# Recurrence preparation of both second-block layers moved from the mixer program into the projection program, in another row order, with key norms per token

## Chip, cores and metric

The kernel runs on one NeuronCore of a Trainium2 chip, as one launch. The metric is the device time of that launch in microseconds (us); lower is better. The time before is 3351.52 us, the median of three runs (3350.27 to 3356.59).

## The reference, cut to what matters

The program computes a first block (a state space mixer, long convolutions and a mixture over 16384 small experts) and then a second block of two layers (l = 0 and 1) on 256 tokens of width 1024. Only the second block is touched. Each of its layers projects the normed tokens to 1216 columns `za`, 416 columns `zb` and 512 columns `zc`. These feed three mixers: a gated recurrence (on za), a latent attention (on zb) and a spatial gate (on zc). After them come an output projection and a feed-forward part. What the change moves is the beginning of the recurrence, up to its loop:

```python
def rwkv7_time_mix(za, shift_mu, w0, w_up, a0, a_up, g_up, k_k, k_a, r_k, ln_g, ln_b, v_first, v0, v_down, v_up):
    za = token_shift(za, shift_mu)
    r, k, v, wd, ad, gd = jnp.split(za, A_SPLITS, axis=-1)      # 3 x 384, 32, 32, 64 columns
    w_log = -jax.nn.softplus(-(w0 + jnp.tanh(wd) @ w_up)) - 0.5
    decay = jnp.exp(-jnp.exp(w_log.astype(jnp.float32)))
    a = jax.nn.sigmoid(a0 + ad @ a_up)
    g = jax.nn.sigmoid(gd) @ g_up
    if v_first is not None:                                      # layer 1 only
        v = v + (v_first - v) * jax.nn.sigmoid(v0 + (v @ v_down) @ v_up)
    kk = heads(k * k_k)                                          # 6 heads of 64
    kk = kk / jnp.maximum(jnp.sqrt(jnp.sum(kk * kk, axis=-1, keepdims=True)), 1e-12)
    k = k * (1 + (a - 1) * k_a)
    ...                                                          # the recurrence over 256 tokens
```

## The kernel before, in words

Here l is the layer, PE the TensorE, DVE the VectorE, ACT the ScalarE, POOL the GpSimd and SP the engine whose queue issues the loads. `second_layer` (L3739) runs the layer as a chain of programs ("stages"), each with one instruction list per engine. A stage ends in a barrier over all engines (`Stage.__exit__`, L115), so no engine starts the next stage before all have finished this one. Order within an engine is the order of the code, and engines wait on each other's semaphores.

**`stage_norm_z`, the projection (L1966 to L2123).** It norms the tokens (ACT squares L2038, DVE L2082 to L2086), transposes them (PE L2014) and splits them into high and low halves hh and hl. Then it multiplies ten weight tiles "row by row": for each of the ZT = 10 tiles of 128 za columns ACT rounds the weights to a high half (L2046), DVE subtracts to get the low half (L2091), PE makes 3 x 8 matmuls (L2024), ACT evicts (L2067), and DVE applies the token shift (L2111, L2112). The tiles come in order: r (3 tiles), k (3), v (3), and last the low-rank tile (wd, ad, gd). Two tiles are in flight. After them come eight units, one for each 128 rows of depth, each with 416 columns of zb and 512 of zc (PE L2032, ACT L2054 and L2055, DVE L2095 and L2096, two units ahead). At the end ACT copies zc (L2075) and DVE zb (L2122) from PSUM.

**`stage_mixers` (L2126 to L2879).** Its first part, before PE's first `fill`, prepares the recurrence and the attention:
- ACT: gelu of zc (L2476), tanh and sigmoid of the low-rank tile (L2477, L2478), squares of the keys (L2480), sigmoids of the lifted tiles (L2484, L2485), the value gates for l = 1 (L2488 to L2491), roots (L2495, L2498), three exponentials (L2500 to L2502).
- PE: lifts of the low-rank tile (L2347), key norms as a product with a 128 x 128 matrix of ones per head (L2353), value lifts (L2359, L2363), transposes of zb (L2371), the attention's projections (L2381, L2385).
- DVE: the latent norms (L2614 to L2618, L2648 to L2652), the centring for the gate (L2621 to L2623), rope angles (L2626 to L2633), the scan over decays (L2642), a reciprocal of the 128 x 768 norms (L2658), key and removal products (L2659 to L2664), value mixing for l = 1 (L2668 to L2670), and the eight writes of AT, BT, KT and RT into block-diagonal tiles (L2678 to L2681).
- POOL: zero fill of the five block-diagonal tiles (L2268). SP: 17 or 19 loads (L2241 to L2260).

Then comes the chunked recurrence as "phases" of three PSUM banks each. PE fills a bank with four matmuls (`fill`, L2408; transposes L2406), and either DVE (`empty`, L2695, L2697) or ACT (`keep_banks`, L2541) reads it. The order is AB, NT, BH, KH, AT, V, KA, RB, RK, then five levels of W, M and T (14 phases, 42 banks), then Q, X and Z. After each bank an engine's list calls `next(attend, None)`: that issues one slice of the attention and the spatial gate ("the side work"). PE's side work is set at the first level (33 slices, first transposes L2282), DVE's at KA (L2708 onward). Between NT and KA, DVE builds the starts TT and Tm of the inverse (L2780 to L2782) and norms the heads (L2775, L2786; ACT L2535, L2548). A sequential loop over four chunks, group norms and transposes end the stage (L2444 to L2472).

Buffers: the preparation's temporaries lie in block-diagonal tiles that are used later. `shared` (L3742) holds attention data and then the output weights.

## Time and profile before

| | |
|---|---|
| median of the runs (3) | 3351.52 us |
| the profiled execution's own time / its span | 3357.79 / 3356.1 us |
| PE / DVE / ACT busy over the span | 3086.5 (92%) / 2430.1 (72%) / 1762.9 (53%) us |
| layer 0: projection / mixers | about 1462 to 1523 / 1524 to 1688.5 us |
| layer 1: projection / mixers | about 1929 to 1992 / 1994 to 2174 us |

The profile is one execution, taken by the hardware profiler. Busy times of the engines overlap, so they don't add up to the span. "Idle before" in a row is the engine's wait ahead of that group and what ended it. The weight loads (PEld) run beside the matmuls. PEclk is the clock that TensorE was granted, as a share of 2.4 GHz; 0.5 is the lower of its two levels, 1.2 GHz. The other 2900 us belong to the first block, the dense feed-forward part and the mixture of experts, which the change doesn't touch.

### The profile page before, as it was taken

The page shows a single profiled execution, that of the slowest core. Times are in us where ns is not written, and L with a number is a line of the kernel's source. Part 1 is how long each engine was busy: PE and PEld are TensorE (multiplying, and loading weights), DVE is VectorE, ACT ScalarE, POOL GpSimd, SP SyncE. Part 2 cuts the span into 40 slices and gives each one's busy share as a digit, 9 for nine tenths or more (in the row PEclk, how much of TensorE's full clock was granted, in tenths as well). Part 3 has the DMA queues.
Part 4 walks back from the last instruction along what each step waited for, and adds up shares of the span by engine and source line. Part 5 has one row for each costly group of instructions (what it writes and reads, how often), then busy time and mean ns, then how long its engine had stood idle before and what let it go on. Part 6 is the DMA issues. An engine that isn't in the chain of part 4 may idle for free. (4 is left out here: it accounts for less than half of the span.)

```text
span 3356.1 us, 49912 instructions
## 1 busy us (share of the span) xinstructions
PE 3086.5 (92%) x17008; PEld 2574.3 (77%) x17009; DVE 2430.1 (72%) x3665; ACT 1762.9 (53%) x2206; POOL 39.8 (1%) x47
## 2 busy tenths in 40 slices
PE   7999898889899999977979986879999999999997
PEld 3797546888788999965859866758888888888886
DVE  3665654899788666658645467559889888988986
ACT  3344303436533444435224344248887887888886
POOL 0000000000000000000000000000000000000000
PEclk9998798999999999988989987979999999999999
DMA  7561133345577666631135240169999999999994
GB/s 276 201 226 35 72 135 116 130 148 182 220 250 220 218 212 212 201 115 46 51 129 181 103 155 1 57 232 390 374 357 377 367 360 367 373 363 351 387 366 173
DMA packets 225998, 732.47 MB, mean 218 GB/s; under 512 B 23543, under 2 KB 59816, under 8 KB 223016
## 3 DMA queue, kind: packets, MB, share of 16 engines
q1 hardware_dynamic: 221928, 702.85, 57.2%
q0 software_dynamic: 2768, 23.59, 2.4%
q10 hardware_dynamic: 1152, 4.19, 0.3%
q8 instruction: 74, 1.21, 0.1%
q14 instruction: 76, 0.62, 0.1%
HBM read 702.76 MB, written 28.84 MB: 218 GB/s over the span
## 5 line engine op out<-in xcount | busy, mean ns | idle before, releaser
L3351 DVE TENSOR_TENSOR moe_lo<-moe_raw,moe_hi 128x1024 fp32r<-128x1024 f32 x756 | 886.1, 1220 | 66.5 <-ACT moe_hi L3201 42.7
L3201 ACT ACTIVATE moe_hi<-moe_raw 128x1024 fp32r<-128x1024 f32 x756 | 789.6, 1061 | 151.7 <-PE moe_pB L3149 83.1
L3149 PE MATMUL moe_pB<-moe_hi,moe_hEh 128*128 128x512 f32 x1008 | 399.9, 397 | 2.6 <-DVE moe_hEl L3346 2.6
L3149 PE MATMUL moe_pB<-moe_hi,moe_hEl 128*128 128x512 f32 x1008 | 394.2, 391 | 0.0
L3149 PE MATMUL moe_pB<-moe_lo,moe_hEh 128*128 128x512 f32 x1008 | 393.6, 390 | 0.0
L1547 PE MATMUL route_pS<-fh,route_uh 128*128 128x256 f32 x640 | 191.2, 299 | 36.0 <-DVE route_ul L1650 35.7
L3149 PEld LDWEIGHTS moe_pB<-moe_hi,moe_hEh 128*128 128x128 f32 x1008 | 190.0, 189 | 40.5 <-issue 2.8
L3149 PEld LDWEIGHTS moe_pB<-moe_hi,moe_hEl 128*128 128x128 f32 x1008 | 189.7, 188 | 40.7
L3149 PEld LDWEIGHTS moe_pB<-moe_lo,moe_hEh 128*128 128x128 f32 x1008 | 190.3, 189 | 38.0
L1882 PE MATMUL exp_pO<-exp_vh,exp_ah 128*128 128x512 f32 x512 | 201.1, 393 | 4.2 <-DVE exp_al L1941 4.2
L1882 PE MATMUL exp_pO<-exp_vl,exp_ah 128*128 128x512 f32 x512 | 200.6, 392 | 0.0
L1882 PE MATMUL exp_pO<-exp_vh,exp_al 128*128 128x512 f32 x512 | 199.8, 390 | 0.0
L3167 PE MATMUL moe_pB<-moe_hi,moe_ah 128*128 128x512 f32 x504 | 196.6, 390 | 0.0
L1905 ACT ACTIVATE exp_vh<-exp_vs 128x1024 fp32r<-128x1024 f32 x128 | 135.1, 1056 | 116.4 <-PE exp_pO L1882 94.3
L3167 PE MATMUL moe_pB<-moe_lo,moe_ah 128*128 128x512 f32 x504 | 196.1, 389 | 0.0
L3167 PE MATMUL moe_pB<-moe_hi,moe_al 128*128 128x512 f32 x504 | 196.1, 389 | 0.0
L1930 DVE TENSOR_TENSOR exp_vl<-exp_vs,exp_vh 128x1024 fp32r<-128x1024 f32 x128 | 156.4, 1222 | 41.1 <-ACT exp_vh L1905 39.8
L1547 PE MATMUL route_pS<-fl,route_uh 128*128 128x256 f32 x640 | 185.6, 290 | 0.0
L1547 PE MATMUL route_pS<-fh,route_ul 128*128 128x256 f32 x640 | 185.4, 290 | 0.0
L1547 PEld LDWEIGHTS route_pS<-fh,route_uh 128*128 128x128 f32 x640 | 127.1, 199 | 40.7 <-DVE route_ul L1650 29.8
L1870 PE MATMUL exp_pS<-fh,exp_ul 128*128 128x256 f32 x512 | 144.9, 283 | 0.0
L1870 PE MATMUL exp_pS<-fl,exp_uh 128*128 128x256 f32 x512 | 144.9, 283 | 0.0
(752 smaller groups left out, 6784.5 us busy)
## 6 DMA issues: line engine op xcount, KB each, us to landing
moe_raw<-in_moe_w SPq DMA_DIRECT2D x758, 512.0 KB, 6.0
exp_vs<-in_peer_v SPq DMA_DIRECT2D x128, 512.0 KB, 4.4
route_us<-in_peer_u SPq DMA_DIRECT2D x64, 512.0 KB, 3.5
exp_us<-in_peer_u SPq DMA_DIRECT2D x64, 512.0 KB, 4.8
inp_w<-in_w_mod SPq DMA_DIRECT2D x48, 512.0 KB, 6.2
inp_w<-in_w_tiles SPq DMA_DIRECT2D x40, 512.0 KB, 6.1
gates<-route_big POOLq DMA_DIRECT2D x8, 2048.0 KB, 8.8
exp_gs<-gates SPq DMA_DIRECT2D x32, 512.0 KB, 5.6
```

What stands on the lines that cost most here:

```text
L1547: m = pe.matmul(pS[:, n % 2, 0:T], w, x[:, kd], start=kd == 0 and q == 0, stop=kd == KD - 1 and q == 2)
L1870: m = pe.matmul(pS[:, j % 2, 0:T], w, x[:, kd], start=kd == 0 and q == 0, stop=kd == KD - 1 and q == 2)
L1882: m = pe.matmul(pO[:, a, h], w[:, j % RING, ts], x, start=False, stop=False, skip_group_check=True)
L1905: act.activation(vh[:, j % RING], vs[:, j % RING], ACT.Copy).then_inc(vh_ready, 1)
L1930: dve.tensor_tensor(vl[:, j % RING], vs[:, j % RING], vh[:, j % RING], ALU.subtract).then_inc(vl_ready, 1)
L3149: i = pe.matmul(pB[:, kind], l[:, kd], m[:, n % HALVES, ns], start=kd == 0 and x == 0, stop=kd == KD - 1 and x == 2)
L3167: i = pe.matmul(pY[:, h], l[:, u], m[:, n % HALVES, hs], start=g == 0 and u == 0 and x == 0, stop=g == GROUPS - 1 and u == UNITS - 1 and x ...
L3201: act.activation(hi[:, n % HALVES], raw[:, n % RING], ACT.Copy).then_inc(hi_ready, 1)
L3351: dve.tensor_tensor(lo[:, n % HALVES], raw[:, n % RING], hi[:, n % HALVES], ALU.subtract).then_inc(lo_ready, 1)
```

## The change

For both layers (in words, the core of the diff follows):
- **Row order.** The low-rank tile is projected first, then k, r, v (`ORDER`).
- **Moved into the projection stage.** tanh after row tile 1 and sigmoid after tile 2 (counted from 0, ACT); the lifts on PE after tiles 4, 5 and 6, with their sigmoids and the copy of g on ACT; key scaling and squares on ACT at tile 7; the norms on PE after tile 8; decay scan, exponentials, key and removal products, the value gates and value mixing (l = 1), the latent norms, and the block-diagonal writes between the units; gelu of zc directly from PSUM at the end. The POOL zero fills (with one more for the reset row of the scan) and the loads for all this move too.
- **zb and zc apart.** Instead of 8 units of 928 columns there are 16: first 8 of zb (416 columns), then 8 of zc (512), four ahead instead of two. The zc weights now lie in the ring of row weights, so their load waits for the last row tile.
- **Key norms per token.** Instead of 3 matmuls of 128 x 128 by 256 columns, 3 roots of 128 x 256 and a 128 x 768 reciprocal, there are 6 matmuls with 2 columns, one root and one reciprocal of 128 x 12, a spread to 128 x 768 on ACT and 6 transposes on PE.
- **Mixer stage.** PE begins with 6 transposes of zb and goes straight to the fills. The attention's projections (8 slices, PE and ACT) lie between the banks of BH, KH and AT. Centring and rope angles come after the build of TT and Tm. The head norms (reduction and scaling) become slices of DVE's side work, which begins at RK instead of KA; PE's begins at level 1 instead of level 0. ACT starts with the twelve diagonal tiles (before: L2531, after the attention's projections).

```diff
+    RING, AHEAD, WIDE_AHEAD = 4, 2, 4
+    LOW = ZT - 1
+    ORDER = [LOW, *range(AT, 2 * AT), *range(AT), *range(2 * AT, 3 * AT)]
+    UNITS = [(n, kd) for n in range(2) for kd in range(KD)]
+    WIDTH = (B_COLS, C_COLS)
+    BQKV = BQL + BKVL
+    NM, W3 = AT * NCH, AT * T
+    RATE = math.exp(-0.5)
+    UP_AT, SQUARE_AT, NORM_AT = 4, 7, 8
...
+                sp.dma_start(wu[:], up).then_inc(up_loaded, 16)
+                sp.dma_start(pre["po"][:], pair_ones).then_inc(po_loaded, 16)
...
+                sp.wait_ge(wl_ready, ZT)
+                sp.dma_start(wc, w_c).then_inc(c_loaded, 16)
+                sp.dma_start(pre["mk"][:], masks).then_inc(mk_loaded, 16)
+                sp.wait_ge(mk_loaded, 16)
...
+            @block.gpsimd
+            def _(pool):
+                pool.memset(rst[:], 1.0).then_inc(zeroed, 1)
+                for n in ("AT", "BT", "KT", "RT", "VT"):
+                    pool.memset(pre[n][:], 0.0).then_inc(zeroed, 1)
+                pool.wait_ge(zeroed, 1)
+                pool.memset(chunks(rst[:])[:, :, 0:1], 0.0).then_inc(zeroed, 1)
...
+                def norms():
+                    pe.wait_ge(norm_in, 1)
+                    pe.wait_ge(po_loaded, 16)
+                    pe.wait_ge(up_read, AT)
+                    for a in range(TT):
+                        for j in range(AT):
+                            i = pe.matmul(pt[:, 1, (a * AT + j) * 2:(a * AT + j) * 2 + 2], t1[:, j, a * P:(a + 1) * P], pre["po"][:, 0:P:HD], start=True, stop=True)
+                    i.then_inc(norm_psum, 1)
...
+                def spread_out():
+                    pe.wait_ge(spread_ready, 1)
+                    for j in range(AT):
+                        for a in range(TT):
+                            at = (a * AT + j) * P
+                            i = pe.transpose(pt[:, j // 2, j % 2 * T + a * P:j % 2 * T + (a + 1) * P], spread[:, at:at + P], k.ident[:])
+                    i.then_inc(spread_psum, 1)
+
+                def values():
+                    pe.wait_ge(v_loaded, 32)
+                    pe.wait_ge(kk_ready, 1)
+                    pe.wait_ge(za_ready, ZT + 1)
...
+                    if UP_AT <= n < UP_AT + AT:
+                        lifted(n - UP_AT)
+                    if n == NORM_AT:
+                        norms()
...
+                for u, (what, kd) in enumerate(UNITS):
+                    pe.wait_ge(bl_ready, u + 1)
...
+                    if u == 1:
+                        spread_out()
+                    if l and u == 5:
+                        values()
+                    if l and u == 7:
+                        values_up()
...
+                def squares():
+
+                    act.wait_ge(za_ready, 1 + 1 + AT)
+                    for j in range(AT):
+                        act.activation(kk[:, j], kx[:, j], ACT.Copy, scale=k.col(f"kk{l}", j, 1))
+                        i = act.activation(t1[:, j], kx[:, j], ACT.Square, scale=k.col(f"kk{l}", j, 1))
+                    i.then_inc(norm_in, 1)
...
+                def spreads():
+                    act.wait_ge(inverse_ready, 1)
+                    act.activation(spread.rearrange("p (n e) -> p n e", e=HD), ni[:].rearrange("p a n -> p (a n)").unsqueeze(2).to_broadcast([P, TT * 2 * AT, HD]),
+                                   ACT.Copy).then_inc(spread_ready, 1)
+
+                def exps():
+                    act.wait_ge(scan_ready, 1)
+                    act.wait_ge(spread_psum, 1)
+                    act.activation(e1, L, ACT.Exp, scale=-RATE).then_inc(exp_ready, 1)
+                    act.activation(e2[:], L, ACT.Exp, scale=RATE).then_inc(exp_ready, 1)
+                    act.wait_ge(scan_ready, 2)
+                    act.activation(lw[:], lw[:], ACT.Exp, scale=-RATE).then_inc(exp_ready, 1)
...
+                        high_wide(2 * (n + AHEAD - ZT))
+                        high_wide(2 * (n + AHEAD - ZT) + 1)
+                    if n == 1:
+                        tanh()
+                    if n == 2:
+                        gate()
+                    if UP_AT <= n < UP_AT + AT:
+                        lifted(n - UP_AT)
+                    if n == SQUARE_AT:
+                        squares()
+                    if n == SQUARE_AT + 1:
+                        kept()
+                act.wait_ge(norm_psum, 1)
+                act.activation(nr[:].rearrange("p a n -> p (a n)"), pt[:, 1, 0:TT * 2 * AT], ACT.Sqrt).then_inc(norm_root, 1)
+                spreads()
+                for u in range(WIDE_AHEAD, 2 * KD):
+                    high_wide(u)
+                    if u == 5:
+                        exps()
+                    if l and u == 10:
+                        value_low()
+                    if l and u == 12:
+                        value_gates()
+                    if u == 13:
+                        b_squares()
+                b_roots()
+                act.wait_ge(b_used, 2 * KD)
+                act.activation(zc[:], pc[:], ACT.Gelu)
...
+                def inverse():
+                    dve.wait_ge(norm_root, 1)
+                    c.link(dve.tensor_scalar(nr[:], nr[:], 1e-12, None, ALU.max))
+                    dve.reciprocal(ni[:], nr[:]).then_inc(inverse_ready, 1)
+
+                def scaled_keys():
+                    dve.wait_ge(spread_psum, 1)
+                    c.tick(dve.tensor_tensor(kk[:, 0:2], kk[:, 0:2], pt[:, 0].rearrange("p (j t) -> p j t", t=T), ALU.mult))
+                    dve.tensor_tensor(kk[:, 2], kk[:, 2], pt[:, 1, 0:T], ALU.mult).then_inc(kk_ready, 1)
+
+                def keys():
+                    dve.wait_ge(kx_scale, 1)
+                    c.tick(dve.tensor_tensor(kx, t2, kx, ALU.mult))
+
+                def removal():
+                    dve.wait_ge(kk_ready, 1)
+                    c.settle()
+                    c.tick(dve.tensor_tensor(aa[:], aa[:], kk[:], ALU.mult))
...
+                inverse()
+                steps = {4: (scan,), 5: (keys,), 6: (scaled_keys,), 7: (removal,)}
+                for u in range(WIDE_AHEAD, 2 * KD):
+                    low_wide(u)
+                    for step in steps.get(u, ()):
+                        step()
+                    if u == 8:
+                        ends()
+                    if u >= 9:
+                        placed(("AT", "BT", "KT", "RT")[(u - 9) // 2], HALVES[(u - 9) % 2])
+                b_means()
+                placed("RT", HALVES[1])
+                b_scaled()
+                if l:
+                    mixed()
...
-            @block.gpsimd
-            def _(pool):
-                for n in ("AT", "BT", "KT", "RT", "VT"):
-                    i = pool.memset(bd[n][:], 0.0)
-                i.then_inc(q["zeroed"], 1)
...
-                pe.wait_ge(q["up_loaded"], 16)
-                pe.wait_ge(q["low_ready"], 2)
-                for j in range(AT):
-                    for n, (lo, hi) in enumerate(((0, 32), (32, 64), (64, 128))):
-                        src = zaT[lo:hi, 9, :] if n == 1 else lt[lo:hi, :]
-                        i = pe.matmul(UP[n][j], wu[lo:hi, j * P:(j + 1) * P], src, start=True, stop=True)
-                    if j:
-                        i.then_inc(q["up_psum"], 1)
-                pe.wait_ge(q["norm_in"], 1)
-                pe.wait_ge(q["po_loaded"], 16)
-                for j in range(AT):
-                    i = pe.matmul(NORM[j], po_[:], t1[:, j, :], start=True, stop=True)
...
                 attend = iter(())
                 fill("AB", "AT", "BT")
                 fill("NT", "BT", "AT")
...
+                attend = lifted()
...
-                attend = side()
                 for n in range(LEVELS):
+                    if n == 1:
+                        attend = side()
...
-                c.link(dve.tensor_scalar(t1[:], t1[:], 1e-12, None, ALU.max))
-                c.link(dve.reciprocal(t1[:], t1[:]))
-                c.link(dve.tensor_tensor(kk, kk, t1[:], ALU.mult))
...
-                attend = side()
...
                 empty("KA", "KA", mask=LT_)
                 empty("RB", "RB", mask=LE_)
+                attend = side()
```

## Rows read from the trace of the kernel before

**Rows 1.** Stretches: us, busy (instructions) of PE, PEld, DVE, ACT, POOL, PEclk, DMA share, GB/s
```profile
1462.00:1524.10 62.10, 54.57 (x352) 50.03 (x352) 37.20 (x60) 28.55 (x50) 0.00 (x0) 0.92 0.38 146
1524.10:1558.50 34.40, 20.37 (x54) 11.51 (x54) 32.08 (x53) 24.02 (x54) 6.68 (x5) 0.65 0.36 112
1558.50:1591.00 32.50, 25.47 (x200) 24.15 (x200) 28.02 (x43) 12.92 (x23) 0.00 (x0) 0.95 0.00 1
...
1993.80:2041.20 47.40, 23.09 (x66) 12.91 (x66) 35.37 (x55) 23.45 (x50) 6.65 (x5) 0.64 0.25 82
...
1577.00:1591.00 14.00, 8.32 (x48) 7.16 (x48) 13.79 (x30) 0.00 (x0) 0.00 (x0) 0.88 0.01 1
```

**Rows 2.** DVE in order of time, preparation of layer 0: start, us, group
```profile
1536.53 1.76 DVE L2642 TENSOR_TENSOR_SCAN rw_L<-rw_V,rw_At 128x768 f32<-128x768 f32 x1 [0.45 <-ACT rw_At L2485]
...
1541.70 4.95 DVE L2658 RECIPROCAL rw_t<-rw_t 128x768 f32<-128x768 f32 x1
```

**Rows 3.** ACT and DVE in order of time, projection of layer 0
```profile
1492.18 0.39 ACT L2067 ACTIVATE z_raw<-z_pz 128x256 f32<-128x256 f32 x1 [1.59 <-PE z_pz L2024]
...
1495.05 0.39 ACT L2067 ACTIVATE z_raw<-z_pz 128x256 f32<-128x256 f32 x1 [1.53 <-PE z_pz L2024]
1495.33 1.05 ACT L2046 ACTIVATE z_wh<-z_w 128x1024 fp32r<-128x1024 f32 x1
...
1515.78 0.68 DVE L2096 TENSOR_TENSOR z_bl<-z_wc,z_bh 128x512 fp32r<-128x512 f32 x1
...
1522.08 1.02 DVE L2122 COPY zb<-z_pb 128x832 f32<-128x832 f32 x1 [2.89 <-PE z_pc L2032]
```

**Rows 4.** PE in order of time, layer 0, and layer 1 (last row)
```profile
1518.26 0.35 PE L2032 MATMUL z_pb<-z_bh,z_hl 128*128 128x416 f32 x1
1518.45 0.40 PE L2032 MATMUL z_pc<-z_bh,z_hh 128*128 128x512 f32 x1
1518.68 0.39 PE L2032 MATMUL z_pc<-z_bl,z_hh 128*128 128x512 f32 x1
...
1530.96 0.79 PE L2347 MATMUL rw_q<-zaT,rw_Kh 32*128 32x256 f32 x1
...
1533.25 0.79 PE L2347 MATMUL rw_p<-rw_Kh 32*128 32x256 f32 x1
...
2008.10 1.50 PE L2359 MATMUL rw_q<-zaT,rw_Kh 128*16 128x256 f32 x6
```

**Rows 5.** POOL and DVE in order of time, start of the mixers, both layers
```profile
1525.11 0.94 DVE L2614 TENSOR_TENSOR heads<-zb 128x768 f32<-128x768 f32 x1
...
1528.19 1.30 DVE L2618 TENSOR_SCALAR rw_mla_s<-rw_mla_s 128x2 f32<-128x2 f32 x1
...
1999.10 1.37 POOL L2268 MEMSET rw_VT<- 128x1536 f32 x1
...
1996.82 3.67 DVE L2617 TENSOR_SCALAR rw_mla_s<-rw_mla_s 128x2 f32<-128x2 f32 x1
```

**Rows 6.** ACT in order of time, preparation of layer 0
```profile
1526.80 1.28 ACT L2478 ACT_TABLE_LOAD   x1
1528.10 0.41 ACT L2478 ACTIVATE rw_Kh<-zaT 64x256 f32<-64x256 f32 x1
```

**Rows 7.** PE in order of time, layer 0: attention projections, two phases of fills
```profile
1553.78 1.24 PE L2381 MATMUL rw_m<-heads,rw_mla_co 128*128 128x288 f32 x4
1554.85 0.81 PE L2385 MATMUL rw_m<-heads,rw_mla_co 128*128 128x384 f32 x2
...
1561.29 2.84 PE L2408 MATMUL rw_q<-rw_AT,rw_BT 128*128 128x128 f32 x24
1563.97 2.84 PE L2408 MATMUL rw_q<-rw_RK,rw_BT 128*128 128x128 f32 x24
```

**Rows 8.** DVE, layer 0, 1560 to 1645 us, by line: xcount | busy, mean ns | idle before
```profile
L2786 DVE TENSOR_TENSOR heads<-heads,rw_mla_h 128x2304 f32<-128x2304 f32 x1 | 2.6, 2558 | 0.0
L2775 DVE TENSOR_REDUCE rw_mla_h<-heads 128x24 f32<-128x2304 f32 x1 | 2.5, 2543 | 0.0
```

499 lines of the change are left out of this document (250 added, 249 removed).

## The prediction

> **What bounds the kernel now.** I read the page first, then the stretches of the two second-block layers, then the engines in order of time in them, last their waits. 92% busy says that TensorE (PE) sets the pace nearly everywhere; the stretches show where it doesn't. Layer 0's projection keeps PE busy 54.57 of 62.10 us. The mixers then open with 34.40 us (layer 1: 47.40) in which PE is busy 20.37 (23.09), and that at a mean granted clock of 0.65 (0.64): mostly the lower of its two levels, 1.2 GHz, so a warm PE would need about two thirds of it. DVE is busy 32.08 of the 34.40 us [rows 1]. So this preparation, 81.8 us over both layers, is a DVE and ACT chain; its longest link is a reciprocal of 4.95 us on 128x768 norms, its next the scan, 1.76 us [rows 2]. In the projection, DVE and ACT have room beside a row tile of 2.87 us: ACT needs 0.39 and 1.05 [rows 3]. The change uses that room.
>
> The sum goes stage by stage, against the profiled execution (3357.79 us, span 3356.1), which lies 6.3 us above the median of the runs. I carry the difference over to the median.
>
> **Projection, start.** PE's first transposes wait for the tokens' norm on DVE, which uses tensor_scalar operations. The six POOL fills now begin at the same barrier: five of 1.37 us and a shorter one, 7.5 us in all. In the mixers a tensor_scalar on two columns took 1.30 us next to such a fill, and in layer 1 one took 3.67 us, until the last fill ended. A product of two tensors beside the fills took 0.94 us, as usual [rows 5]. In the projection three such operations stand in a chain, from 2.2 us after the barrier. Bounds: 0, if each slips between two fills, and 5.5 us, if all wait for the last one. I take 3.5 us per layer, between one fill of wait for each (about 3) and the 3.67 row. The Trainium skill, "SBUF — State Buffer", section "SBUF: two separate sides", has the shared port pair held by whoever starts first "for the whole instruction", so one wait should last one fill at most, and the layers would pay about 3 us each, which makes the sum 1 us smaller; the 3.67 us row says that waits can be longer.
>
> **Projection, row tiles.** The reordering costs nothing. The lifts are new for PE here: from one to the next took 2.29 us at the low clock [rows 4], so 1.15 warm, three times: 3.5 us. tanh and sigmoid (0.4 us each and a table load of 1.28 [rows 6]) bring ACT's load beside one tile to 3.1 us, about the tile, and the two-tile lead covers it. At tile 7 ACT gets six operations of about 0.43 us: raw and high half 1.4, then 2.6, so the norms on PE, due 2.9 us after tile 7, start at 4.2: wait 1.3, then 1.4 for six full weight loads.
>
> **Projection, zb and zc.** From the end of tile 7 (t = 0): tile 8 and norms to 5.6, tile 9 to 8.5, two zb units (six matmuls of 0.19 us [rows 4], 1.15) to 10.8. PE then waits for root (table load), inverse and spread, one chain ACT-DVE-ACT, until 13.0: 2.2 us; six transposes 0.7. Units 2 to 7 need 6.9 us of PE, but the scan (1.76), its subtraction and products of 0.96 stand on DVE between the low halves, and three exponentials of 0.8 on ACT: last zb unit at 22.3. Then come eight zc units: PE 6 x 0.23 = 1.4 each, DVE 0.68 plus a block-diagonal write of 0.94 [rows 3, 5], so 1.6 each, to 35. The last write and the scaled latents make 37.4. Before, from the same point (eviction at 1495.05) to the end of the zb copy (1522.08 + 1.02) it was 28.1 [rows 3]. Layer 0: +9.3 us.
> In layer 1 PE also runs the value lifts. They took 1.50 us each [rows 4], and they wait for the key norms, which lets go of the bank (1.5 us), and for an ACT copy queued behind unit 10's high half; then three mixing products of 0.98 us at the end of DVE's list. End 42.8: +14.7.
> Projection in all: 3.5 + 3.5 + 9.3 = +16.3 for layer 0, and +21.7 for layer 1. The loads (576 KB of masks, the later zc weights) land before use: the zc weights have 16 us.
>
> **Mixers.** The preparation goes: -34.4 and -47.4 us. Left are six transposes of zb and their wait, 1.7 us each.
> The fills pay for it. From AB to the first side transposes it took 32.5 us [rows 1]. A phase of fills takes 2.68 us (1561.29 to 1563.97), a group pair of attention projections 1.7, four times [rows 7]. Walk: AB, NT 5.4; BH, KH, AT 6.7 with projections 6.8, to 18.9; V 1.3; 1.3 of wait, since ACT squares the heads (2.1 us) ahead of V's banks; KA, RB and one bank of RK 6.3: 27.8. TT and Tm, centring and angles hide under that: DVE needs about 16 us to there. Then DVE bounds. Its side work before KA's end ran in 1577 to 1591: 13.79 us busy [rows 1], less nine bank reads of 0.62 is 8.2. Now the head reduction and scaling join (2.54 + 2.56 [rows 8], 0.5 for small ones), and eleven bank reads: 8.2 + 5.6 + 6.8 = 20.6. First side transposes at 48.6, against 32.5: +16.1. To that comes the clock: PE has stood for 3 to 6 us at the stage's edge, and if it starts at 1.2 GHz, as the 0.65 row suggests, AB and the transposes cost up to 4.5 us more; I take 2.5 and 4 us.
> PE's side work begins nine banks later and still has its 33 banks, so nine banks without side work vanish at the end: 9 x 0.89 = -8.0.
> Layer 0: -34.4 + 1.7 + 16.1 + 2.5 - 8.0 = -22.1. Layer 1: -47.4 + 1.7 + 16.1 + 4.0 - 8.0 = -33.6.
>
> **Sum.** 16.3 + 21.7 - 22.1 - 33.6 = -17.7 us. That is 3340.1 as the profiled execution, and 3351.5 - 17.7 = 3333.8 for the median; I say 3334. Of 81.8 us of preparation a fifth is gained.
>
> **Rivals.**
> *B, the waits are absorbed.* POOL slips in (-7), the clock stays up at the edge (-6.5), and the 1.3 + 2.2 + 1.8 us of waits in each projection, with layer 1's 1.5, overlap better than in my walk (-12): 26 us more, 3308. For it: the bounds themselves. Against: the 3.67 us row, and that the waits are chains of single operations.
> *C, slower: the clock falls inside the projection.* From the spread on, PE is busy 7.6 of 13.8 us up to the last zb unit. In 1577 to 1591 it was busy 8.32 of 14.00 and the mean clock was 0.88 [rows 1], so it fell for a part. If it falls here and stays low through the zc units, these take 2.8 instead of 1.4 us: 8 x 1.4 = 11.2, and about 3 more on the zb units and tile 9, 14 a layer, 28 in all: 3334 + 28 = 3362. It decides if PE is still at 1.2 GHz when the fourth zc unit begins. Against: the zc units then keep PE full, and full stretches stood at 1.00.
> *D, the move only relabels.* The projection's end has no cover left: POOL at its worst (+4), clock at its worst (+2.5), and ACT's chain of loads, root, spread and exponentials (4 us a layer) adds to PE's work instead of overlapping: +14.5, 3348, no change. For it: DVE and ACT both hand every unit on, and each added step stands in their one queue. The Trainium skill, "ScalarE: Activation LUTs", section "What ACT_TABLE_LOAD costs", gives 2.66 us for every switch of table set. Here the load took 1.28 us, and the next operation began 0.02 us after it [rows 6]. By the page's figure three switches a layer in the chain would add an estimated 8 us; the trace speaks against it.
>
> **How the numbers follow.** Forecast 0.52, B 0.23, D 0.14, C 0.11. About 0.2% (6.7 us) is what a measurement of this kernel can tell from no change. Faster by more: forecast and B, 0.75; within: D, 0.14; slower: C, 0.11. The range goes from B's 3308 to 3355, which takes in D and the lesser forms of C; C's full price and a better B are left out.
>
> **What would show it.** In the changed profile: no DVE reciprocal of 128x768; the fill AB within 3 us of the mixers' first instruction (right), or after a wait (wrong: something moved isn't finished). The projection's norm tensor_scalars longer than before (POOL). PE idle ahead of its six two-column matmuls and ahead of the spread's transposes, 1 to 2 us each. Projection of layer 0 about 78 us, of layer 1 about 86. DVE without idle time from RK to T0, and PE waiting there. PEclk below 1 over the zc units would be C. The forecast is wrong if the projections grow by more than 27 us each, or the stretch from AB to the side transposes by less than 8.

## The result, and the profile after

The changed kernel takes 3315.2 us (median of 4 runs, 3312.6 to 3322.1) against 3350.9 (4 runs, 3347.7 to 3356.6) for the kernel before: ratio 0.9895, 95% interval 0.9875 to 0.9915, so 28 to 42 us less. The forecast was 17.7 us less. The direction was right, 3315 lies in the range, and the forecast change was about half of the measured one.

The profiled execution of the changed kernel spans 3313.8 us, 42.3 less than the one of before. Not all of that is the change. I cut both traces at each stage's first SyncE or ACT instruction: the two projections and the two mixers together went from 484.4 to 451.5 us, 32.9 less. (In layer 0 that instruction stands 10 us into the stage behind the mixers, so each such sum holds 10 us of the output projection too. The table below, which ends at the mixers' last DVE operation, doesn't.) The other 9.4 us lie in stages that are the same code (the state-space stage alone took 106.6 and 99.6 us, the routing 366.0 and 362.6). A second trace of the kernel before (below) has 482.8 us in the four stages and 2862.2 in all the rest, where the changed kernel has 2862.3. So the change is worth 31 to 33 us in its own stages, and that is what has to be explained. It is 1.8 to 1.9 times the forecast, where the medians say 2.0 times.

Here are the cuts that answer to the prediction's terms, in us. "AB" is the first fill, "side" the first side transposes, "Q" DVE's first plain copy of a bank (phase Q), "end" the start of the last DVE operation of the mixers. Where the last column has two numbers, they are against the first and the second trace of before.

| | predicted | before | before, again | after | measured |
|---|---|---|---|---|---|
| layer 0: projection | +16.3 | 62.1 | 63.3 | 76.6 | +14.6 / +13.4 |
| start to AB | -32.7 | 34.4 | 34.4 | 0.7 | -33.7 |
| AB to side | +18.6 | 32.5 | 34.2 | 50.3 | +17.8 / +16.1 |
| side to Q | -8.0 | 55.9 | 55.8 | 47.8 | -8.0 |
| Q to end | 0 | 41.1 | 41.1 | 39.5 | -1.6 |
| layer 1: projection | +21.7 | 64.8 | 64.9 | 83.3 | +18.5 / +18.4 |
| start to AB | -45.7 | 47.5 | 47.4 | 1.4 | -46.1 / -46.0 |
| AB to side | +20.1 | 32.6 | 32.6 | 50.9 | +18.4 |
| side to Q | -8.0 | 60.4 | 55.8 | 47.8 | -12.6 / -8.0 |
| Q to end | 0 | 39.5 | 39.4 | 39.5 | 0 |

The stretches of the changed kernel, in the columns of [rows 1]: us, busy (instructions) of PE, PEld, DVE, ACT, POOL, PEclk, DMA share, GB/s. They are layer 0's projection, AB to side, side on; then layer 1's projection, AB to side, side on.

```profile
1453.40:1530.07 76.67, 61.61 (x388) 53.63 (x388) 54.25 (x86) 48.84 (x90) 8.52 (x7) 0.91 0.37 133
1530.79:1581.08 50.29, 41.79 (x299) 38.42 (x297) 37.72 (x66) 23.01 (x51) 0.00 (x0) 0.93 0.21 56
1581.08:1628.00 46.92, 46.04 (x402) 45.55 (x403) 33.13 (x77) 16.83 (x52) 0.00 (x0) 1.00 0.08 25
...
1909.73:1993.03 83.30, 64.60 (x400) 55.74 (x400) 57.25 (x89) 52.68 (x96) 8.52 (x7) 0.91 0.34 123
1994.39:2045.32 50.93, 42.44 (x298) 39.06 (x297) 37.72 (x66) 21.65 (x48) 0.00 (x0) 0.92 0.17 55
2045.32:2085.00 39.68, 38.80 (x337) 38.30 (x338) 28.00 (x67) 16.10 (x50) 0.00 (x0) 1.00 0.01 2
```

The preparation's stretch of [rows 1] (34.40 us with PE busy 20.37) is gone. Layer 0's projection keeps PE busy 61.61 of 76.67 us and DVE 54.25, where before it was 54.57 and 37.20 of 62.10. The shape is the predicted one: a projection 15 us longer, no preparation, a DVE-bound stretch ahead of the side transposes.

PE in order of time, layer 0 of the changed kernel: the two lifts that follow each other, the norms, the spread's transposes, and the start of the mixers (start, us, group, [idle before and what ended it]).

```profile
1480.85 0.37 PE L2071 MATMUL z_pt<-z_lt,z_wu 32*128 32x256 f32 x1
1485.15 0.37 PE L2071 MATMUL z_pt<-z_lt,z_wu 32*128 32x256 f32 x1
...
1497.31 1.50 PE L2080 MATMUL z_pt<-pre_po,z_sq 128*128 128x2 f32 x12 [0.97 <-ACT z_sq L2160]
1506.02 0.88 PE L2088 MATMUL z_pt<-ident,z_xn 128*128 128x128 f32 x6 [2.01 <-ACT z_xn L2186]
...
1530.11 0.85 PE L2581 MATMUL rw_m<-ident,zb 128*128 128x128 f32 x6 [3.24 <-PEq L119]
1530.79 4.47 PE L2621 MATMUL rw_q<-pre_BT,pre_AT 128*128 128x128 f32 x24
```

The trace has two instructions for each f32 product, so x12 are the six two-column products, which took 1.50 us (predicted 1.4). A tile with a lift takes 4.30 us from one lift to the next, so a lift costs 1.4 (predicted 1.15). PE waits 0.97 us for the squares (predicted 1.3) and 2.01 for the spread (predicted 2.2). AB follows the first transposes by 0.7 us and takes 4.47 us instead of the 2.84 of a warm phase [rows 7]: the cold start, 1.6 us.

DVE, layer 0: the norm at the projection's start, and the stretch that sets the time before the side transposes.

```profile
1455.68 1.18 DVE L2270 TENSOR_SCALAR z_ms<-z_ss 128x2 f32<-128x2 f32 x1 [1.48 <-ACT z_sq L2137]
1457.13 0.17 DVE L2272 RECIPROCAL z_rs<-z_rt 128x2 f32<-128x2 f32 x1 [0.27 <-ACT z_rt L2139]
1457.33 3.25 DVE L2274 TENSOR_SCALAR z_xn<-x_tok,z_rs 128x1024 f32<-128x1024 f32 x2
...
1559.93 0.69 DVE L2811 TENSOR_TENSOR rw_RK<-rw_q,pre_mk 128x512 f32<-128x512 f32 x1 [0.20 <-PE rw_q L2621]
1560.54 0.16 DVE L2823 TENSOR_SCALAR rw_gm_c<-rw_gm_c 128x2 f32<-128x2 f32 x1
1560.83 0.69 DVE L2811 TENSOR_TENSOR rw_RK<-rw_q,pre_mk 128x512 f32<-128x512 f32 x1
1561.44 2.54 DVE L2826 TENSOR_REDUCE rw_mla_h<-heads 128x24 f32<-128x2304 f32 x1
...
1568.74 2.56 DVE L2841 TENSOR_TENSOR heads<-heads,rw_mla_h 128x2304 f32<-128x2304 f32 x1
```

From 1559.9 to 1581 DVE has no gap, as predicted, and PE waits for it: 7.6 us in all in this waits view of PE, 1559 to 1582 us (us in total, times, longest).

```profile
PE rw_q L2621 <- DVE pre_VT L2811: 3.8, 3, 2.4
PE rw_q L2621 <- DVE rw_RK L2811: 1.4, 1, 1.4
PE rw_q L2621 <- DVE rw_TT L2813: 1.3, 1, 1.3
PE rw_m L2519 <- DVE heads L2856: 1.1, 1, 1.1
```

### The profile page after: what moved, and what is told of

Same layout as the page of the kernel before. It is cut to its first block and busy times, and to the rows that moved or that the text cites. A ratio compares the mean times of both kernels' runs of the same rounds, so it can differ in the third digit from the quotient of the medians.

```text
span 3313.8 us, 49981 instructions
## 1 busy us (share of the span) xinstructions
PE 3068.4 (93%) x17032; PEld 2563.2 (77%) x17033; DVE 2407.7 (73%) x3642; ACT 1778.0 (54%) x2242; POOL 43.6 (1%) x51
## 5 line engine op out<-in xcount | busy, mean ns | idle before, releaser
L3333 ACT ACTIVATE moe_hi<-moe_raw 128x1024 fp32r<-128x1024 f32 x756 | 789.7, 1061 | 151.0 <-PE moe_pB L3281 81.8
L1547 PE MATMUL route_pS<-fh,route_uh 128*128 128x256 f32 x640 | 190.8, 298 | 34.4 <-DVE route_ul L1650 34.1
L1547 PEld LDWEIGHTS route_pS<-fh,route_uh 128*128 128x128 f32 x640 | 126.3, 197 | 39.4 <-DVE route_ul L1650 29.4
```

What stands on the lines that cost most here:

```text
L1547: m = pe.matmul(pS[:, n % 2, 0:T], w, x[:, kd], start=kd == 0 and q == 0, stop=kd == KD - 1 and q == 2)
L3333: act.activation(hi[:, n % HALVES], raw[:, n % RING], ACT.Copy).then_inc(hi_ready, 1)
```

## The experiments

The four changed stages repeat far better from trace to trace than the whole time does, so each run is read by their cuts, with the ratio to the kernel before beside it. "Four stages" is their sum: 484.4 and 482.8 us before, 451.5 after. "Mixers" runs from their first instruction to "end" of the table, where nothing else is said: 138.3 and 139.6 us in the changed kernel. "Raw" is ACT's eviction of a row tile. Each run has one trace, so a difference in one cut is worth something only where it is larger than what equal code shows from trace to trace.

**What is the kernel, what is the execution.** The kernel before, run again.

> The kernel before, once more, for a second trace. The changed kernel's trace is 42 us shorter than the first one, but only 33 us of it lie in the two projections and mixers; 9 us lie in stages that were not touched (7.0 of them in the state-space stage, 106.6 against 99.6 us, and 3.4 in the routing). Theory 1 (those 9 us are one execution against another): the stage of 106.6 us comes out otherwise here, and the two projections and mixers repeat within 1 us each. Rival (the untouched stages differ by program): 106.6 us again. For layer 1's mixers: PE ran 11.2 us at a mean clock of 0.58 from the first side transposes on. If that belongs to the kernel before (its preparation of 47 us keeps PE half idle), it stands here again and the stretch from the side transposes to the last DVE operation takes 99 us; if it was chance, it takes 94 to 95.

Measured: ratio 1.0006 (0.9997 to 1.0016). State-space stage 99.6, so theory 1: the 9 us outside are one execution against another. Inside the four stages the cuts repeat within 0.2 us but for three: layer 0's projection (+1.2), its AB to side (+1.6), and layer 1's "side to Q", which is 55.8 us, not 60.4. The first trace of before has this row where PE starts its side work (columns as above):

```profile
2073.82:2085.00 11.18, 11.18 (x60) 11.07 (x61) 3.17 (x6) 1.98 (x4) 0.00 (x0) 0.58 0.01 2
```

PE was at 1.2 GHz for most of 11 us there. In the second trace it was not. So 4.6 of the 32.9 us were a fall of the clock in one execution of the old kernel. Two more traces have the old layer 1 mixers from there on: 55.8 us again in one, 57.5 in the other (layer 0 alone, next), with its own shorter fall. The change can't be credited with it.

**Is the gain the sum of two layers.** In both kernels one layer uses the old functions under other names (here layer 1, in the second kernel layer 0):

```diff
     with ExitStack() as mixer:
...
+    if l == 1:
+        old_norm_z(...); old_mixers(...)
+    else:
         stage_norm_z(...); stage_mixers(...)
```

> The change in layer 0 alone, layer 1 as before. The forecast on record has -5.8 us for this half. Theory 1 (each layer gains by itself what its stages show in the changed kernel's trace: projection +14.6, preparation -33.7, first side transposes +17.8, the rest -9.7): -11 us, layer 1 as in the kernel before. Rival (the layers lean on each other, the clock that layer 1 finds depends on what layer 0 did): layer 1's mixers here take other than the 181.8 us of before by 4 us or more.

> The change in layer 1 alone, layer 0 as before. The forecast on record has -11.9 us for this half. Theory 1: projection +18.5, preparation -46.1, side transposes +18.4, the rest -12.7, in all -22 us; both halves add up to the -33 us of the whole. Rival: the halves overlap or need one another, and their sum misses -33 by 5 us or more.

Measured: layer 0 alone 0.9968 (0.9956 to 0.9980), 10.7 us; four stages 475.2, 7.7 to 9.2 less. Layer 1 alone 0.9940 (0.9927 to 0.9953), 20.1 us; four stages 462.3, 20.5 to 22.1 less. They add to 30.8 us by the times. There is no sign that the layers lean on each other: with layer 0 changed, layer 1's mixers take 180.9 us up to the next stage, between the 181.8 and 177.2 of the two traces of before.

**Undoing the placement.** The move stays; the attention part goes back to where it was.

```diff
-                fill("AB", "AT", "BT")
-                fill("NT", "BT", "AT")
-                attend = lifted()
+                for _ in lifted():
+                    pass
+                attend = iter(())
+                fill("AB", "AT", "BT")
+                fill("NT", "BT", "AT")
...
+                attend = side()
                 for n in range(LEVELS):
-                    if n == 1:
-                        attend = side()
```

(and on ACT and DVE the same orders as before: centring and rope angles ahead of the first banks, head sums before KA, the diagonal tiles behind the projections).

> The changed kernel with the attention part placed as before: its projections ahead of the first fill, the head reduction and scaling between the fills NT and KA, DVE's side work from KA on and PE's from level 0 on. By the steps of the forecast the fills AB come 6.8 to 9 us later, the first side transposes some 33 us after AB instead of 50, and nine banks at the end carry no side work less: mixers from first instruction to last DVE operation within 3 us of the changed kernel's 138.3 us a layer (138 to 143). Theory 1 (the placement is worth little, the gain is the preparation's cover in the projection): 138 to 143. Rival (the placement between the fills is what I under-priced, 7 us a layer): 146 or more a layer, and 3330 us in all.

Measured: 0.9967 (0.9955 to 0.9979), mixers 148.4 and 150.1 us: the rival. Undoing the placement costs 10.0 and 10.6 us. My expectation fell on one number: AB begins 16.5 us after the stage, not 8 to 10. The waits view of PE, 1529 to 1547 us:

```profile
PE rw_m L2594 <- DMA heads<-in_w_ukv: 6.9, 1, 6.9
```

PE waits 6.9 us (layer 1: 6.0) for the projections' weights, whose loads are issued when the stage begins. The mean clock from start to AB is 0.69. In the kernel before, PE had no such wait: the preparation covered the landing. In the changed kernel AB and NT cover it: its first projection begins 8.6 us into the stage (1538.67), without a wait.

To see whether it is the load, the two weights go first in SP's queue:

```diff
+                sp.dma_start(wq, w_uq).then_inc(q["m_w_loaded"], 16)
+                sp.dma_start(wkv, w_ukv).then_inc(q["m_w_loaded"], 16)
                 sp.dma_start(posi[:], ...)
...
-                sp.dma_start(wq, w_uq).then_inc(q["m_w_loaded"], 16)
-                sp.dma_start(wkv, w_ukv).then_inc(q["m_w_loaded"], 16)
```

> The kernel with attention placed first, its two weight loads (576 and 384 KB) put ahead of the stage's other loads on SP's queue; there PE waited 6.9 us for them, and AB came 16.5 us after the stage began. Theory 1 (the placement between the fills is worth 10 us a layer because AB and NT cover the landing of these weights): AB comes at 14.5 to 15 us, as the loads are issued 1.9 us earlier. Rival (another load, or the chain of evictions on ACT, holds the projections anyway): within 0.5 us of 16.5.

Measured, in a single execution: start to AB 15.5 and 13.9 us instead of 16.5 and 16.8, and PE's wait for the weights went from 6.9 to 5.1 and from 6.0 to 3.7 us. So AB follows the load, as theory 1 has it, but by 1.0 us in layer 0, less than expected, and by 2.9 in layer 1. Nothing here takes the whole wait away; that the loads account for all of it is read from the waits view.

**Undoing the norms per token.**

```diff
-                            i = pe.matmul(pt[:, 1, (a * AT + j) * 2:(a * AT + j) * 2 + 2], t1[:, j, a * P:(a + 1) * P], pre["po"][:, 0:P:HD], ...)
+                    for j in range(AT):
+                        i = pe.matmul(pt[:, j // 2, j % 2 * T:(j % 2 + 1) * T], pre["po"][:], t1[:, j, :], ...)
...
-                    c.link(dve.tensor_scalar(nr[:], nr[:], 1e-12, None, ALU.max))
-                    dve.reciprocal(ni[:], nr[:]).then_inc(inverse_ready, 1)
+                    c.link(dve.tensor_scalar(spread, spread, 1e-12, None, ALU.max))
+                    c.link(dve.reciprocal(spread, spread))
```

> The changed kernel with the key norms taken as before: three products with the 128x128 matrix of ones, roots, bound and reciprocal on 128x768, and no spreading and transposing. Theory 1 (DVE's queue is what ends the projection from the scan on, so the reciprocal's 4.95 us, less the small inverse, lands on the end): projections longer by 3.5 to 5 us each, 80 to 82 and 87 to 88; 7 to 10 us in all. Rival (PE's units cover it): each within 1 us of 76.6 and 83.3.

(DVE's product with the norms also moves up, right behind the scan.) Measured: 0.9934 (0.9918 to 0.9951); projections 84.3 and 89.7 us, +7.7 and +6.4. Theory 1, and more than it said. Layer 0: DVE's reciprocal, PE's wait behind it, and the stretch after (columns as above).

```profile
1505.06 4.95 DVE L2296 RECIPROCAL z_xn<-z_xn 128x768 f32<-128x768 f32 x1
```

```profile
1510.69 0.71 PE L2124 MATMUL z_pb<-z_bh,z_hh 128*128 128x416 f32 x1 [5.32 <-DVE z_bl L2281]
```

```profile
1503.00:1511.00 8.00, 2.68 (x14) 2.33 (x14) 6.75 (x5) 2.22 (x5) 0.00 (x0) 0.95 0.07 30
1511.00:1520.00 9.00, 5.62 (x15) 4.33 (x15) 6.18 (x8) 5.51 (x8) 0.00 (x0) 0.50 0.00 0
```

DVE's 5 us become a PE wait of 5.32, and then PE runs at 1.2 GHz for 9 us (layer 1 has the same, 0.50 over 9 us). That second part is what rival C of the prediction describes.

**Undoing both: the move alone.**

> The changed kernel with both helpers undone at once: key norms by column, and the attention part placed as before. What is left of the change is the move of the preparation into the projection. Measured one at a time, undoing the norms cost 14.1 us (7.7 + 6.4) and undoing the placement 20.6 us (10.0 + 10.6) of stage time. Theory 1 (the two prices add, and the move by itself gains next to nothing): 34.7 us slower than the changed kernel by its stages, about 3349 us, within 0.2% of the kernel before. Rival (they overlap, since both leave PE idle and cold; the move by itself keeps a good part of the 31 us): 3335 us or less.

Measured: 3351.1 against 3348.6, ratio 1.0008 (0.9999 to 1.0017); four stages 483.5, against 484.4 and 482.8 before, and 32.0 us above the changed kernel where theory 1 had 34.7. Theory 1. Moving 82 us of preparation into the projections gains nothing by itself. Layer 0, in cuts: the projection grows by 22.3 us (to 84.3), start to AB shrinks by 18.4 (to 16.0, since load and projections are now bare), and "side to Q" grows by 3.2 (59.1). That last part stands at the start of PE's side work, here in this kernel and in the one before:

```profile
1587.27:1592.00 4.73, 4.73 (x32) 4.68 (x32) 1.24 (x2) 1.19 (x2) 0.00 (x0) 0.71 0.00 0
```

```profile
1591.07:1596.00 4.93, 4.93 (x44) 4.93 (x45) 2.07 (x4) 1.19 (x2) 0.00 (x0) 1.00 0.00 0
```

PE is busy in both, but at 0.71 it does 1.4 us less. The rest is waits for DVE behind it: 3.5 us in all instead of 2.0 up to Q. The kernel with the placement undone has the same, 59.2 us with 4.4 us of waits and 0.68 over its first 4.7 us. So 3 of the 10 us that the placement is worth there lie behind the side transposes; why the clock stands lower there, no run tells.

**The two helpers without the move.** First the norms per token in the kernel before: the same two-column products, spread and transposes, in its own preparation.

```diff
-                c.link(dve.tensor_scalar(t1[:], t1[:], 1e-12, None, ALU.max))
-                c.link(dve.reciprocal(t1[:], t1[:]))
-                c.link(dve.tensor_tensor(kk, kk, t1[:], ALU.mult))
+                dve.wait_ge(q["spread_psum"], 1)
+                c.tick(dve.tensor_tensor(kk[:, 0:2], kk[:, 0:2], M[0][:].rearrange("p (j t) -> p j t", t=T), ALU.mult))
...
```

> The kernel before with the key norms per token in its own preparation (twelve two-column products, roots, bound and inverse on 128x12, spread by ACT, six transposes), nothing moved. In the changed kernel the norms by column cost 7.7 and 6.4 us, because the reciprocal of 4.95 us stood in DVE's queue ahead of PE's operands. Theory 1 (in the kernel before the same reciprocal stands on the same kind of DVE chain, so this part of the change was worth its 5.4 us of DVE less 0.4 without any move): the first fill comes 4 to 5 us earlier in each layer (29.5 to 30.5 instead of 34.4, 42.5 to 43.5 instead of 47.4), 8 to 10 us in all. Rival (the round trip DVE, ACT, PE, DVE takes the reciprocal's place as a wait): less than 2 us a layer.

Measured: 0.9973 (0.9962 to 0.9983), 9 us; AB comes at 32.9 and 43.4 us instead of 34.4 and 47.4, 5.5 us in all by the cuts (7 and 5 by the four stages). Theory 1 in layer 1 (4.0 us), the rival in layer 0 (1.5). In layer 0 DVE ends its last block write 29.9 us into the stage instead of 34.3, the 4.4 us of theory 1, but then this stands in the way:

```profile
1544.60 0.96 DVE L2694 TENSOR_TENSOR rw_RT<-zaT,rw_e 64x768 f32<-64x768 f32 x1
```

```profile
1547.14 0.81 PE L2394 MATMUL rw_m<-heads,rw_mla_co 128*128 128x384 f32 x2
1548.59 1.60 PE L2417 MATMUL rw_q<-rw_BT,rw_AT 128*128 128x128 f32 x12 [0.64 <-ACT rw_mla_v L2537]
```

In layer 0 the attention projections, which had been hidden under DVE, now end last. Then the placement in the kernel before:

```diff
-                pe.wait_ge(q["m_c_read"], TT)
...
+                def lifted(): ...
                 pe.wait_ge(q["bd_ready"], 1)
...
                 fill("NT", "BT", "AT")
+                attend = lifted()
```

> The kernel before with the attention part placed as in the changed kernel (projections under the fills BH to AT, head sums and scaling in DVE's side work, side work from RK and level 1), the preparation where it was. In layer 0 PE waited 2.87 us for DVE's last block-diagonal write, after its projections were done; in layer 1 DVE was done at 2036.4 and PE began AB at 2041.3. Theory 1 (the placement pays only where nothing else covers the projections and the landing of their weights, so it needs the move): the first fill comes at 34.4 as before in layer 0 and 4 to 5 us earlier in layer 1, AB to the side transposes grows by 17 to 18 us, the stretch behind shrinks by 8: slower by 9 to 10 us in layer 0 and 4 to 6 in layer 1, 3363 us or so. Rival (the placement is good by itself, as its 10 us a layer in the changed kernel suggest): faster than before by 8 us or more.

Measured: 1.0034 (1.0021 to 1.0047), 11 us slower; theory 1. AB at 34.3 and 42.5 us, AB to side 51.6 and 51.4 (+19), side to Q 47.8 (-8). PE's waits of layer 0 before AB:

```profile
PE rw_q L2412 <- DVE rw_RT L2693: 15.6, 1, 15.6
```

The same placement gains 10 us a layer in one kernel and costs 10.5 and 1.3 us in the mixers of the other (8.9 and 5.8 against the second trace of before). There DVE's preparation must still end before AB, so taking the projections away from before AB saves 0.1 us in layer 0 and 5 in layer 1, while AB to side grows by 19. What decides is whether something else covers the weights' landing and the projections.

**The prediction's small waits.** POOL's fills held back:

```diff
             def _(pool):
+                pool.wait_ge(hl_ready, KD // 2)
                 pool.memset(rst[:], 1.0).then_inc(zeroed, 1)
```

> The changed kernel with POOL's seven fills of the projection held back until DVE has written the low halves of the normalised tokens, so that they lie beside the row tiles. Theory 1 (the fills hold DVE's tensor_scalar operations, as the forecast had it at 3.5 us a layer): the norm's three operations are short again (0.17, 0.17, 1.42 us), the first raw eviction comes at 12.6 us instead of 15.6 in layer 0, and the projections shrink by 3.0 us (layer 0, to 73.6) and 1.0 to 3.0 (layer 1, to 80.3 to 82.3). Rival (DVE pays the same elsewhere: the fills now hold its work in the row tiles): the row tiles grow from 2.9 us by 0.5 or more each and the projections stay within 1 us of 76.6 and 83.3.

Measured: 0.9899 (0.9882 to 0.9916), projections 76.5 and 83.9 us: no gain, but not by the rival's reason. The norm is short again, and DVE's row-tile operations beside the fills keep their 0.43, 0.48 and 1.23 us:

```profile
1459.38 0.17 DVE L2271 TENSOR_SCALAR z_ms<-z_ss 128x2 f32<-128x2 f32 x1 [1.99 <-ACT z_sq L2138]
...
1460.02 1.42 DVE L2275 TENSOR_SCALAR z_xn<-x_tok,z_rs 128x1024 f32<-128x1024 f32 x2
...
1474.89 0.48 DVE L2365 SCALAR_TENSOR_TENSOR zaT<-z_df,cols,z_raw 128x256 f32<-128x256 f32 x1
1475.37 1.23 DVE L2280 TENSOR_TENSOR z_wl<-z_w,z_wh 128x1024 fp32r<-128x1024 f32 x1
```

DVE hands over the tokens 2.8 us earlier (layer 1: 1.8), but the first raw comes only 1.6 us earlier (14.0 instead of 15.6 us into the stage; layer 1: 1.0). PE is at 1.2 GHz when it starts (PEclk 0.50 up to its first row tile), and the moment at which the clock rises within that tile varies from execution to execution of equal code. In the eight traces whose layer 0 norm is short, PE starts that tile 8.9 us into the stage; the clock rises at 10.1 to 10.2 us in four of them and at 13.2 to 13.4 in the other four, and the first raw comes at 12.6 or 14.0. So the fills cost layer 0 1.6 to 3.0 us. Then the last row tile, behind PE's 0.96 us wait for the norms, takes it back: 6.1 us from raw to raw instead of 4.7.

```profile
1499.50:1503.00 3.50, 3.50 (x24) 3.50 (x25) 1.91 (x4) 2.49 (x6) 0.00 (x0) 0.75 0.74 300
1503.00:1506.00 3.00, 3.00 (x19) 2.99 (x19) 0.17 (x1) 0.59 (x2) 0.00 (x0) 0.73 0.95 401
```

The clock fell inside that tile, for 3.4 us in layer 0, and layer 1's took the same 6.2 instead of 4.7 us. In the changed kernel's trace the same place stood at 1.00. But the fall is not this edit's alone: five traces hold the changed projection of layer 1 unaltered, and in two of them (the heads by halves and the loads first, 85.5 us each instead of 82.9 to 83.3) this tile took 6.1 to 6.2 us too. Here it is in the kernel with the heads by halves:

```profile
1956.54:1962.71 6.17, 6.01 (x38) 6.01 (x39) 1.91 (x4) 2.73 (x7) 0.00 (x0) 0.72 0.92 355
```

In layer 0 none of five such traces has it. Whether bringing PE forward causes the fall is therefore open. Next, the norms earlier:

```diff
-    UP_AT, SQUARE_AT, NORM_AT = 4, 7, 8
+    UP_AT, NORM_AT = 4, 7
...
                     if UP_AT <= n < UP_AT + AT:
                         lifted(n - UP_AT)
-                    if n == SQUARE_AT:
-                        squares()
+                        squares(n - UP_AT)
```

(with the root after tile 8 on ACT and the inverse after tile 8 on DVE).

> The changed kernel with the squares one by one after the three lifts instead of all at tile 7, PE's norms after tile 7, root and inverse after tile 8. Theory 1 (PE's two waits, 0.97 before the norms and 2.01 before the spread's transposes, are on the path, as the forecast had them at 1.3 and 2.2): both go, and the projections shrink by 2 to 3 us each, to 73.6 to 74.6 and 80.3 to 81.3. Rival (from the scan on DVE sets the end and has been waiting for nothing PE does): less than 1 us each.

Measured: 0.9885 (0.9868 to 0.9901), projections 73.2 and 80.6, -3.4 and -2.7: theory 1. Of the two waits only this is left, from the end of tile 7 to the end of the stage:

```profile
1507.20 0.46 PE L2125 MATMUL z_pb<-z_bh,z_hh 128*128 128x416 f32 x1 [0.51 <-DVE z_bl L2281]
```

From the first raw on, both layers are 3.3 to 3.4 us shorter; the 0.7 us less in layer 1 is a later first raw (16.75 instead of 16.05). So both waits were on the path, at nearly the sizes predicted. The heads by halves (DVE's part; ACT squares them by halves too):

```diff
+                for a in range(TT):
+                    dve.wait_ge(q["m_squared"], a + 1)
+                    c.tick(dve.tensor_reduce(h1[:, a * NHH:(a + 1) * NHH], qs[:, a], AX_X, ALU.add))
+                c.settle()
                 empty("KA", "KA", mask=LT_)
```

> The changed kernel with the squares and sums of the attention heads in two halves by token block: ACT squares the first half before the AT banks, DVE sums both halves in its idle time ahead of KA. Theory 1 (from RK to the first side transposes DVE sets the time, 20 us of work and waits without a gap): 2.5 us less of DVE work there, and PE's wait of 0.99 for V's banks halves: AB to side transposes 50.3 to 50.9 becomes 47 to 48 us, 3 us a layer. Rival (the sum before KA only delays the reads of KA to RK by as much): within 1 us of 50.3 to 50.9.

Measured: 0.9894 (0.9877 to 0.9910). AB to side 48.5 and 48.4 (-1.8, -2.6), side to Q 49.4 instead of 47.8 in both: the mixers gain 0.2 and 0.9 us. Theory 1 in the stretch, though it said 47 to 48, and twelve mixers of equal code took 49.3 to 50.9 us there. Then it is given back at the start of PE's side work:

```profile
1582.00:1586.00 4.00, 3.22 (x16) 3.13 (x17) 2.38 (x6) 0.59 (x1) 0.00 (x0) 0.61 0.00 0
```

This too has happened without the edit: in the kernel with layer 1 alone changed, AB to side took 49.3 us and side to Q 49.4, with a mean clock of 0.57 over the first 4 us of side work.

**Together, and better than both.**

> The changed kernel with the fills later and the norms earlier, both in the projection. Alone, the first brought the first row eviction 1.6 and 1.0 us forward and lost it again to 3.4 us of PE at 1.2 GHz in the last row tile, behind PE's wait for the norms; the second took that wait away and gained 3.4 and 2.7 us. Theory 1 (the fall of the clock hung on that wait): both gains add, 71.7 and 79.6 us, 8.6 us in all, 3306 us. Rival (the fall comes with the earlier start, wait or none): 73.2 and 80.6 as with the norms alone.

> The same, and in the mixers the squares and sums of the attention heads by halves, with the product of the gate's weights and its triangle ahead of KA too. Alone, the halves took 1.8 and 2.6 us off the stretch from AB to the first side transposes and gave 1.6 back behind it, where PE ran its first 4 us of side work at a mean clock of 0.61. Theory 1 (that fall of the clock stays): 0.5 to 2 us a layer better than the kernel with the two in the projection. Rival (with the further 0.7 us of DVE taken away PE's waits are short enough and the clock stays up): 3 to 4 us a layer better, about 3299 us.

Measured: fills and norms together 3306.4 us, 0.9875 (0.9860 to 0.9890), projections 70.4 and 78.95; with the heads too (and the gate's weight product ahead of KA) 3304.6, 0.9870 (0.9855 to 0.9885), projections 71.7 and 78.1, mixers 136.6 and 136.7 instead of 138.3 and 138.4. In the first kernel the last row tile takes 2.85 us from raw to raw, which is a plain tile at the full clock. In all six projections with the norms earlier (three kernels, two layers) no fall comes there, and the gains add, as theory 1 said: 6.2 and 4.4 us, for 5.0 and 3.7 one by one. The 1.2 and 0.7 us on top lie in the clock's rise in the first row tile again (first raw at 12.6 us in layer 0; with the heads too, at 14.0). The four stages take 439.6 and 436.7 us, 12 and 15 less than the changed kernel's. The heads gain 1.7 us a layer in the mixers, 1.4 over projection and mixers, theory 1 of that run; in layer 0 the mean clock was still 0.64 over the first 3.9 us of side work.

## Why the prediction was right in direction and half the size

**Right.** The order of the steps and nearly every mechanism: the preparation's stretches vanish (predicted -32.7 and -45.7, measured -33.7 and -46.1); DVE bounds the time from RK to the side transposes (the walk says 48.6 us, though its own terms, 27.8 and 20.6, add to 48.4; measured 50.3 and 50.9 with a cold start); nine banks without side work vanish at the end (-8.0, measured -8.0 in layer 0 against both traces and in layer 1 against the second); the waits at the norms and the spread (1.3 and 2.2, measured 0.97 and 2.01) were on the path, as the run with the norms earlier showed. The projections came within 1.7 and 3.2 us.

**Where the missing 15 us are.** Against the trace I forecast from, the misses of the table add to 5.1 us in layer 0 and 9.9 in layer 1. No cut is off by more than 4.6, and none of them errs to the fast side, so they add up instead of cancelling. The mechanism held; the sizes of its terms failed, and these two most.
- *The step that failed most is the clock.* "I take 2.5 and 4 us" for a cold start, and nothing for what the old kernel itself lost. The cold start cost 1.7 and 2.3 against the walk, 2.5 less in all. What I put at nothing, without a reason, is that PE's clock also fell in the kernel before: 4.6 us in layer 1's side work (in that execution), 1.6 in layer 0's Q to end (41.1 in four traces of four with the old order of fills and side work, at a mean clock of 0.87; 39.5 in nine of eleven with the new, at 0.91, but 43.4 in the other two, at 0.80, so this one is no sure gain). I read layer 0's rows for the end of the mixers and carried -8.0 over to layer 1. Together these are 8.7 of the 15 us.
- *The projections* came out 4.9 us too long in the walk, in two terms. *Their start*, +3.5 a layer: PE's first transposes came 2.8 and 1.8 us later in every trace with the fills at the start, so the delay itself was priced too high. Measured by the first raw it is +3.0 in layer 0 (12.6 to 15.6 us) and +1.0 in layer 1 (15.0 to 16.1); against the second trace of before it is +1.6 and +1.0, since part of the delay can vanish in the moment at which the clock rises. *zb and zc*, +9.3 and +14.7: measured to the last DVE operation +7.5 and +13.8. The waits overlapped somewhat better than in the walk. The lifts went the other way, 1.4 instead of 1.15 each.
- The rest is 1.4 us in start to AB, priced at 1.7 us a layer; it took 0.7 and 1.4.

Which term failed most hangs on the trace. Against the second trace of before the misses add to about 13 us: 6.2 in the projections, 2.5 in the cold start, 1.6 in Q to end, 1.6 because AB to side took 34.2 us there, 1.3 in start to AB, and nothing in side to Q. So what is shown against both is 5 to 6 us of overpriced projections and 4 us of clock; the other 4.6 are the luck of one execution.

**What the forecast did not ask.** It booked the gain as "of 81.8 us of preparation a fifth". The runs say otherwise: the move alone is worth 0, the norms per token then 14 us (12 by the four stages), the placement then 21 (20). The walk holds all three, so its sum is not wrong by this, but "of 81.8 us a fifth" books the gain to the one part that earns nothing by itself. I had all three in one walk and never priced one without the others. Had I walked the move with attention first, I would have met the 6.9 us for the weights. The rows of before could not show that wait, because the preparation covered it.

**The rivals.** B (waits absorbed, 3308) came nearest in time, but only part of each of its items came true: fills 3 us of 7, clock 2.5 of 6.5. C (clock falls in the projection): not in the changed kernel's trace, where it stood at 1.00 over the zc units; it did happen in its relatives, for 9 us behind a 5.32 us wait with norms by column, and for some 3.4 us in the last row tile of three more. D (only relabels, 3348) has the time of the move without its two helpers, but not the way to it: the bare weights and the norms by column did most of it, and it had priced neither.

**Fills and table loads.** DVE's tensor_scalar operations beside the fills took 1.0 us more (z_ms) and 1.8 more for the pair (xn), none of them more than one fill (1.4 to 1.9 us). The Trainium skill, "SBUF — State Buffer", section "SBUF: two separate sides", has a holder keep the shared port for one whole instruction; the trace agrees here, and the 3.67 us of [rows 5], which lasted longer than two fills, don't. Each table load of the chain took 1.28 us, as in [rows 6], and the root's load stands 0.02 us from the operations before and after it. The Trainium skill, "ScalarE: Activation LUTs", section "What ACT_TABLE_LOAD costs", makes its 2.66 us of a load of 1.28 and a drain of 1.38; the load agrees, the drain doesn't show here, and the measurement decides.

## What to carry to other kernels

Price each part of a change alone and with the others: a part can be worth nothing, ten or minus ten microseconds by what else covers the same load. When you take work away from the start of a stage, list what it was hiding, the DMAs that are issued at that barrier first. And a forecast made from one trace should look at the granted clock of every stretch that it subtracts from, in both layers, for some of the time lost there is that execution's own.

## What was not expected of the hardware

- Time won ahead of a place can be lost again at that place to the clock, with no instruction in between any different. Two edits that brought PE's work forward by 1.0 to 2.6 us lost 1.5 to 1.6 us behind it, in both layers each, in stretches at mean granted clocks of 0.57 to 0.75. Both falls also came in traces of unaltered code (two of ten projections, one of twelve mixers), against four of four in these two kernels; with all three edits together the second one came in layer 0 alone. So that the edits cause them is likely, not shown. With the 0.96 us wait of PE taken away, the first of them came in none of six projections.
- Norms by column, whose longest link is a reciprocal of 4.95 us on DVE, cost 6.4 to 7.7 us: PE's wait for DVE was followed by 9 us at 1.2 GHz.
- The state-space stage, the same code in all these kernels, took 97 to 107 us from trace to trace. A difference of 10 us between two profiled executions may be no more than that.
- POOL's fills of 128x1536 lengthened DVE's tensor_scalar operations but not its products, its subtractions or its scalar_tensor_tensor operations beside them (0.43, 0.48 and 1.23 us in the row tiles, with fills and without).

Left open: what decides whether and when PE's clock falls or rises at a given place, which these runs only show happening, and with it how much of the gains and losses of 1 to 2 us above each edit owns.
